# Stick-breaking stage of a retention, stick-breaking and expert layer: every second round of TensorE's work in reverse order

## The chip, the cores and the metric

The kernel runs on one core of a Trainium2 chip. The metric is the device time of one execution in microseconds (us), here the median of the runs shown. TensorE is called PE in the profile (its weight loads PEld), VectorE DVE, ScalarE ACT, GpSimd POOL and SyncE SP.

## The reference

One decoder layer on 1024 tokens of width 1024, all in float32. A combined projection gives the inputs of two head groups, retention (4 heads of 128) and stick-breaking attention (8 heads of 64). Their outputs are projected and added to the input; then 32 experts (4 for each token) are added. The change is in the stick-breaking attention, which computes for each block of 128 queries:

```python
z = einsum('bhqd,bhkd->bhqk', q_blk, kt) * scale
causal = key_pos[None, :] < q_pos[:, None]
log_one_minus = where(causal, log_sigmoid(-z), 0.0)
log_remaining = cumsum(log_one_minus, axis=3, reverse=True) - log_one_minus
weights = where(causal, exp(log_sigmoid(z) + log_remaining), 0.0)
out = einsum('bhqk,bhkd->bhqd', weights, vt)
```

Each weight is sigmoid(z) times the product of 1 - sigmoid(z) over the later keys before the query. It is also the difference of two neighbouring running products of 1 - sigmoid(z).

## The kernel before

The kernel is one program with a hand-written order for each engine and semaphores between them. Its stages are the norm and the projections with the retention woven in, the stick-breaking stage, the output projection with the router, and the loop over the experts, which takes most of the time. Each stage waits for the one before it.

**Units.** The stick-breaking stage has 96 units (`NU`, lines 383 to 394). A unit is one head, one block `i` of 128 queries and up to 512 keys. Two heads form a pair `p`; there are 4 pairs. For query blocks 0 to 3 a head has one unit of 1 to 4 key tiles of 128; for blocks 4 to 7 it has two, first the later keys (1 to 4 tiles, with the diagonal), then the first 512 keys. The two heads of a pair alternate, so that units n and n+1 (n even) are the same work for two heads. The 24 units of a pair (`PAIR`) in steps of two have 1, 2, 3, 4, 1, 4, 2, 4, 3, 4, 4, 4 key tiles.

**A unit's way.** It goes through five steps on three engines:
- `scores(n)` on PE (L1001) multiplies queries by keys for units n and n+1. Each product is split in three (high by high, high by low, low by high); each head uses 64 rows of the array. It writes bank n % 4 and bank (n+1) % 4 and increments `z_ok`. From the fifth unit on it waits for `z_not` >= n - 2 (L1007): the sigmoids of units n-4 and n-3, which had the same banks, must be done.
- `remains(n)` on ACT (L763, the operation at L768) takes the sigmoid of -z from the bank into `stick` and increments `z_not`.
- `remaining(n)` on DVE (L1433, L1446) is a scan: the running product from the last key to the first, in `rem`, which increments `z_rem`. The second unit of a query block continues from the first.
- `turn_rest(n)` on PE (L1020, L1027) transposes the 128 x 128 tiles of `rem` into bank 4 + n % 2. It waits for `z_rem` and for ACT to have emptied that bank (`z_wT` >= n - 1).
- `turned(n)` on ACT (L776, L781) copies that bank into `massT`, which has four buffers (n % 4), as 1 minus the value. Therefore it waits for `z_tr` and, from the fifth unit on, for `z_pv` >= n - 3 (L780): the values of unit n-4 must be done.
- `values(n)` on PE (L1030, L1040) multiplies differences of neighbouring value rows, `dv`, by `massT`, for units n and n+1, and adds up in bank 6 or 7. Each head writes 64 partitions. It waits for `z_wT` >= n + 2 and for the rows of `dv`, and increments `z_pv` for each unit.

The differences `dv` are made by POOL (L594) at the start of the stage from DMA copies. DVE copies each finished half of a head pair (`chain_out`, L1449) to the output. ACT copies the next pair's queries and keys in the high precision part (`pair_up`, L770, the operation at L774), DVE subtracts to get the low one (`pair_low`, L1371).

**The order.** ACT runs for n = 0, 2, ... `turned(n-4)`, `turned(n-3)`, `remains(n)`, `remains(n+1)` and at two places of a pair `pair_up` (L786 to L794). DVE runs the scans in the order of the units. PE's order is the loop that is changed (L1049 to L1056): for n = -4, -2, ..., 100 one round is `values(n-6)`, then `turn_rest(n-2)` and `turn_rest(n-1)`, then `scores(n+4)`, each where such units exist.

Of the kernel before, what the change touches and what calls it, by code (L numbers as in the profile page):

```python
# [118 lines left out]
def layer(nc, x, attn_norm_g, w_in, ret_norm_g, sb_q_norm_g, sb_k_norm_g, w_out, ffn_norm_g,  # L119
          w_router, b_router, w_gate_up, b_gate_up, w_down, b_down, consts, rope, out):  # L120
    with ExitStack() as ctx:
# [271 lines left out]
        NU = len(units)  # L393
        PAIR = NU // (SH // 2)

        def out_bank(u):
            return bank[6 + u["chain"] % 2]
# [493 lines left out]
        def _(e):  # L891
# [109 lines left out]
            def scores(n):  # L1001
                u = units[n]
                b, p = u["p"] % 2, u["p"]
                e.wait_ge(z_up, 2 * (p + 1))
                e.wait_ge(z_lo, 2 * (p + 1))
                if n >= 4:
                    e.wait_ge(z_not, n - 2)  # L1007
                queries, keys = slice(u["i"] * P, (u["i"] + 1) * P), slice(u["k0"], u["k0"] + u["w"])
                heads = ((n, slice(0, HD)), (n + 1, slice(HD, P)))
                for m, pr in heads:  # L1010
                    e.matmul(bank[m % 4][:, 0:u["w"]], q_hi[b][pr, queries], k_hi[b][pr, keys], start=True, stop=False,  # L1011
                             skip_group_check=True)
                for m, pr in heads:
                    e.matmul(bank[m % 4][:, 0:u["w"]], q_hi[b][pr, queries], k_lo[pr, p, keys], start=False, stop=False,
                             skip_group_check=True)
                for m, pr in heads:
                    e.matmul(bank[m % 4][:, 0:u["w"]], q_lo[pr, p, queries], k_hi[b][pr, keys], start=False,
                             stop=True, skip_group_check=True).then_inc(z_ok, 1)

            def turn_rest(n):  # L1020
                u = units[n]
                e.wait_ge(z_rem, n + 1)
                if n >= 2:
                    e.wait_ge(z_wT, n - 1)
                for t in range(u["n"]):
                    at = u["at"] + t * P
                    mm = e.transpose(bank[4 + n % 2][:, t * P:(t + 1) * P], rem[:, u["row"], at:at + P], ident)  # L1027
                mm.then_inc(z_tr, 1)

            def values(n):  # L1030
                u = units[n]
                e.wait_ge(z_wT, n + 2)
                e.wait_ge(z_dv, u["i"] + 1)
                if u["chain"] >= 2:
                    e.wait_ge(z_out, u["chain"] - 1)
                cols = slice(u["i"] % HT * P, (u["i"] % HT + 1) * P)
                for t in range(u["n"]):
                    for m, pr in ((n, slice(0, HD)), (n + 1, slice(HD, P))):
                        h = units[m]["h"]
                        mm = e.matmul(out_bank(u)[pr, cols], dv[:, u["k0"] // P + t, h * HD:(h + 1) * HD],  # L1040
                                      massT[m % 4][:, t * P:(t + 1) * P], start=u["diag"] and t == 0,
                                      stop=u["last"] and t == u["n"] - 1, skip_group_check=True)
                        if t == u["n"] - 1:
                            mm.then_inc(z_pv, 1)
# [2 lines left out]
            e.wait_ge(r_mix, NT)  # L1047
            e.wait_ge(r_state, NT)
            for n in range(-4, NU + 6, 2):  # L1049
                if n >= 6:  # L1050
                    values(n - 6)
                if 2 <= n < NU + 2:
                    turn_rest(n - 2)
                    turn_rest(n - 1)
                if n + 4 < NU:
                    scores(n + 4)  # L1056

            e.wait_ge(wo_in, 16)
# [61 lines left out]
            for j in range(NT - 1):  # L1120
                n = NT - 1 - j
# [661 lines left out]
```

## Time and profile before

| | |
|---|---|
| median of 3 runs | 2201.78 us (2200.51 to 2202.93) |
| the profiled execution's own time | 2200.3 us |
| its span, first to last instruction | 2198.4 us |
| granted PE clock, mean | 0.989 |
| PE busy | 97% of the span |
| DVE, ACT, POOL busy | 58%, 35%, 16% |
| stick-breaking stage, first scores to last values | 396.6 to 519.5 us of the span |

The busy shares are means over the whole span. A wait is given with the engine and line that released it. "PEclk" is the share of full speed that PE's clock was granted. "issue" as a releaser means that the profile shows nothing that the engine waited for.

### The profile page before, as it was taken

To read this page: it belongs to the slowest core of one execution; us is meant where nothing else is said; L and a number is where in the kernel's file an instruction comes from. 1 tells how busy PE (TensorE), PEld (TensorE's weight loads), DVE (VectorE), ACT (ScalarE), POOL (GpSimd) and SP (SyncE) were. 2 spreads that over 40 slices of the span, in tenths; PEclk is the share of its full clock that TensorE was granted. 3 is DMA by queue.
4 is the path that set the end of the run, shared out by engine and by line. 5 is a ranking of instruction groups with operands and counts; after the bars stand their busy time and mean duration, and the time that the engine had idled before them with its cause. 6 is when DMAs were issued, how large, how long until landed. Compare 5 with 4: busy or idle time off the path is not lost.

```text
span 2198.4 us, 42048 instructions
## 1 busy us (share of the span) xinstructions
PE 2130.8 (97%) x16443; PEld 1912.0 (87%) x16444; DVE 1274.7 (58%) x2580; ACT 765.8 (35%) x1369; POOL 346.7 (16%) x243
## 2 busy tenths in 40 slices
PE   7999999899979999999999999999999999999997
PEld 6978888677868999899989999989999999999996
DVE  6434534787366665456656655655566665666654
ACT  4143134577222333233333333332333333333332
POOL 3100300200010211111112112111211111212121
PEclk9999999999989999999999999999999999999998
DMA  5221221303365988778879887887898887999983
GB/s 178 95 88 58 96 90 45 116 2 133 136 218 177 315 306 307 241 263 310 311 264 315 307 307 264 308 296 258 310 316 308 307 305 258 317 325 330 315 286 92
DMA packets 257783, 509.59 MB, mean 232 GB/s; under 512 B 7466, under 2 KB 44510, under 8 KB 257438
## 3 DMA queue, kind: packets, MB, share of 16 engines
q1 hardware_dynamic: 234220, 451.95, 57.5%
q0 software_dynamic: 21968, 51.67, 9.6%
q10 hardware_dynamic: 1536, 5.15, 0.7%
q8 instruction: 41, 0.67, 0.1%
q14 instruction: 18, 0.15, 0.0%
HBM read 473.09 MB, written 33.55 MB: 230 GB/s over the span
## 4 chain that ended last, share of the span: by engine, by line
PE 95%; DVE 2%; issue 1%; DMA 1%; POOL 0%; ACT 0%; ACTq 0%; SPq 0%; POOLq 0%; DVEq 0%
PE bank L1217 46%; PE bank L1197 16%; PE bank L928 14%; PE bank L1205 3%; PE bank L1027 2%; PE bank L1040 2%; PE bank L1074 1%; PE bank L1140 1%; PE bank L1076 1%; PE bank L1075 1%; PE bank L1133 1%; PE bank L1011 1%; PE bank L1182 1%; PE bank L1146 1%; PE bank L936 1%
## 5 line engine op out<-in xcount | busy, mean ns | idle before, releaser
L1217 PE MATMUL bank<-hx,ring 128*128 128x140 f32 (+1 forms) x8192 | 1021.9, 287 | 7.5 <-DVEq L1659 7.5
L1217 PEld LDWEIGHTS bank<-hx,ring 128*128 128x128 f32 x8192 | 1015.0, 197 | 10.3 <-DVEq L1659 7.7
L1197 PE MATMUL bank<-work_r,hx_r 128*128 128x512 f32 x1024 | 335.1, 408 | 0.0
L1698 DVE TENSOR_TENSOR mix_r<-ring,work_r 128x1024 fp32r<-128x1024 f32 x256 | 305.1, 1223 | 41.0 <-ACT work_r L853 40.9
L870 ACT ACTIVATE hx<-hx 128x168 f32<-128x168 f32 x256 | 88.0, 344 | 595.8 <-DVE hx L1714 595.6
L1714 DVE TENSOR_SCALAR hx<-bank,small 128x168 f32<-128x168 f32 x256 | 100.3, 392 | 298.6 <-PE bank L1217 289.3
L853 ACT ACTIVATE work_r<-ring 128x1024 fp32r<-128x1024 f32 x256 | 257.7, 1042 | 0.0
L1197 PEld LDWEIGHTS bank<-work_r,hx_r 128*128 128x128 f32 x1024 | 188.1, 189 | 43.8 <-issue 10.4
L1197 PE MATMUL bank<-mix_r,hx_r 128*128 128x512 f32 x512 | 200.1, 391 | 0.0
L630 POOL DMA_INDIRECT out_x<-hx,small x32 | 52.0, 1625 | 659.5 <-ACT hx L863 621.2
L861 ACT ACTIVATE hx<-bank,small 128x512 f32<-128x512 f32 x64 | 44.0, 688 | 313.9 <-PE bank L1146 167.2
L597 POOL DMA_INDIRECT hx<-xn_scratch,small x33 | 33.9, 1029 | 574.1 <-issue 568.0
L876 ACT ACTIVATE hx_r<-hx 128x128 fp32r<-128x128 f32 x256 | 78.8, 308 | 109.0 <-DVE hx L1724 109.0
L928 PE MATMUL bank<-hx_r,mix_r 128*128 128x512 f32 x480 | 112.5, 393 | 3.7 <-DVE hx_r L1308 3.7
L1197 PEld LDWEIGHTS bank<-mix_r,hx_r 128*128 128x128 f32 x512 | 96.1, 188 | 21.0
L928 PE MATMUL bank<-hx_r,work_r 128*128 128x512 f32 x480 | 113.7, 394 | 0.0
L928 PEld LDWEIGHTS bank<-hx_r,mix_r 128*128 128x128 f32 x480 | 89.5, 188 | 23.3 <-issue 5.1
L1619 DVE TENSOR_TENSOR work<-hx,cst 128x3072 bf16<-128x3072 f32 x32 | 107.3, 3352 | 0.0
L928 PEld LDWEIGHTS bank<-hx_r,work_r 128*128 128x128 f32 x480 | 89.7, 188 | 20.2 <-issue 1.9
L633 POOL DMA_INDIRECT out_x<-hx,small x64 | 100.7, 1573 | 19.5 <-issue 19.5
L1716 DVE TENSOR_SCALAR hx<-bank,small 128x168 f32<-128x168 f32 x256 | 98.1, 383 | 0.0
L1633 DVE TENSOR_TENSOR hx<-bank,small 128x512 f32<-128x512 f32 x66 | 42.6, 686 | 86.1 <-PE bank L1140 86.1
(244 smaller groups left out, 2346.8 us busy)
## 6 DMA issues: line engine op xcount, KB each, us to landing
ring<-in_w_gate_up SPq DMA_DIRECT2D x128, 2048.0 KB, 12.9
ring<-in_w_down SPq DMA_DIRECT2D x64, 2048.0 KB, 13.1
mix<-in_w_in SPq DMA_DIRECT2D x14, 1024.0 KB, 5.0
work<-in_w_in SPq DMA_DIRECT2D x14, 1024.0 KB, 5.0
ring<-in_x SPq DMA_DIRECT2D x8, 512.0 KB, 6.0
hx<-in_w_out SPq DMA_DIRECT2D x1, 4096.0 KB, 14.1
work<-in_x ACTq DMA_DIRECT2D x8, 512.0 KB, 4.6
out_x<-work SPq DMA_DIRECT2D x8, 512.0 KB, 4.4
```

Of the source, the lines that this page charges most:

```text
L633: e.indirect_dma_start(out=out_quarters, in_=y_o[:, r], in_offset=None, compute_op=ALU.add, out_offset=bass.IndirectOffsetOnAxis(ap=idx_sc ...
L853: e.activation(dn_hi[:, nh, k:k + 2], dn_ring[:, k:k + 2, nh * CH:(nh + 1) * CH], ACT.Copy).then_inc(c_hi, 1)
L870: e.activation(sg[:, f % 2], g1[:, f % 2], ACT.Sigmoid, scale=GALPHA).then_inc(m_sig, 1)
L876: e.activation(hid_hi[:, f], hid[:, f, 0:P], ACT.Copy).then_inc(h_hi, 1)
L928: mm = e.matmul(dst, lhs, rhs, start=k == 0 and (xs is x_hi and ws is w_hi), stop=k == KD - 1 and ws is w_lo)
L1197: mm = e.matmul(bank[2 + t][:, :], h[:, k], w[:, t, k], start=False, stop=k == KD - 1 and w is dn_lo, skip_group_check=True)
L1205: e.matmul(bank[7][quarter_rows(j), r * 2 * P:(r + 1) * 2 * P], hid[:, k, P + r * OV:P + (r + 1) * OV], dn_ring[:, k, j * 2 * P:(j + 1) * ...
L1217: mm = e.matmul(bank[f % 2][:, part * CAP:part * CAP + w], gu_ring[:, k, f * 256 + part:(f + 1) * 256:2], xT[:, k, 0:w], start=k == 0, sto ...
L1619: e.tensor_tensor(hot, pos_s.unsqueeze(2).to_broadcast([P, NT, NH * P]), slot_at.unsqueeze(1).to_broadcast([P, NT, NH * P]), ALU.is_equal) ...
L1698: e.tensor_tensor(dn_lo[:, nh, k:k + 2], dn_ring[:, k:k + 2, nh * CH:(nh + 1) * CH], dn_hi[:, nh, k:k + 2].bitcast(F32), ALU.subtract).the ...
L1714: e.tensor_scalar(g1[:, b], bank[b][:, 0:CAP], be[:, f:f + 1], GLIM, ALU.add, ALU.min)\
L1716: e.tensor_scalar(u1[:, b], bank[b][:, CAP:2 * CAP], be[:, 8 + f:9 + f], GLIM + 1.0, ALU.add, ALU.min).then_inc(m_up, 1)
```

## The change

In every second round (n = -2, 2, 6, ...) PE does its three kinds of work in the reverse order: scores first, then the turns, then values. In the other rounds nothing changes. The units that a round handles and all instructions and waits are the same. What ACT, DVE, POOL and SP do, and their order, is unchanged.

```diff
             for n in range(-4, NU + 6, 2):
-                if n >= 6:
+                back = n % 4 == 2
+                if back and n + 4 < NU:
+                    scores(n + 4)
+                if not back and n >= 6:
                     values(n - 6)
                 if 2 <= n < NU + 2:
                     turn_rest(n - 2)
                     turn_rest(n - 1)
-                if n + 4 < NU:
+                if back and n >= 6:
+                    values(n - 6)
+                if not back and n + 4 < NU:
                     scores(n + 4)
```

## Rows read from the trace of the kernel before

**Rows 1.** The page: busy time by engine, and the chain that ended last by line.
```profile
PE 2130.8 (97%) x16443; PEld 1912.0 (87%) x16444; DVE 1274.7 (58%) x2580; ACT 765.8 (35%) x1369; POOL 346.7 (16%) x243
...
PE bank L1217 46%; PE bank L1197 16%; PE bank L928 14%; PE bank L1205 3%; PE bank L1027 2%; PE bank L1040 2%; PE bank L1074 1%; PE bank L1140 1%; PE bank L1076 1%; PE bank L1075 1%; PE bank L1133 1%; PE bank L1011 1%; PE bank L1182 1%; PE bank L1146 1%; PE bank L936 1%
```

**Rows 2.** Waits of PE, 380 to 760: us in total, times, longest.
```profile
PE bank L1040 <- POOL ring L594: 4.1, 1, 4.1
```

**Rows 3.** Windows, three pairs: length; PE, PEld, DVE, ACT, POOL busy; clock, DMA share, GB/s.
```profile
418.02:446.56 28.54, 28.38 (x290) 20.95 (x288) 25.00 (x29) 21.16 (x51) 0.00 (x0) 1.00 0.01 2
446.56:475.10 28.54, 28.30 (x290) 20.96 (x288) 24.75 (x29) 21.18 (x51) 0.00 (x0) 1.00 0.01 2
475.10:503.80 28.70, 28.49 (x292) 20.95 (x288) 23.53 (x27) 19.56 (x50) 0.00 (x0) 1.00 0.01 1
```

**Rows 4.** Timeline: start, length, engine, line, work, count, idle before. Rounds of PE.
```profile
441.01 0.19 PEld L1011 LDWEIGHTS bank<-ring_r 64*128 64x128 f32 x2 [0.17 <-issue]
...
441.57 0.64 PEld L1040 LDWEIGHTS bank<-work,ring 128*64 128x64 f32 x12
...
448.61 0.85 PEld L1040 LDWEIGHTS bank<-ring 128*64 128x64 f32 x16 [0.36 <-issue]
...
449.63 0.86 PEld L1027 LDWEIGHTS bank<-cst,work 128*128 128x128 f32 x8 [0.17 <-DVE work L1446]
...
450.33 1.09 ACT L781 ACTIVATE ring<-bank 128x512 f32<-128x512 f32 x2 [1.44 <-PE bank L1027]
450.66 0.19 PEld L1011 LDWEIGHTS bank<-ring_r 64*128 64x128 f32 x2 [0.17 <-issue]
...
451.30 1.10 ACT L768 ACTIVATE work<-bank 128x512 f32<-128x512 f32 x2
451.55 0.42 PEld L1040 LDWEIGHTS bank<-work,ring 128*64 128x64 f32 x8 [0.36 <-ACT ring L781]
```

**Rows 5.** Timeline of the weight loads, router behind eight full-width turns.
```profile
559.02 0.38 PEld L1096 LDWEIGHTS bank<-work,small 128*32 128x32 f32 x16 [0.17 <-issue]
```

**Rows 6.** Timeline of ACT, operations that follow each other without idle time.
```profile
441.66 1.09 ACT L768 ACTIVATE work<-bank 128x512 f32<-128x512 f32 x2
442.61 1.08 ACT L774 ACTIVATE ring_r<-ring 128x1024 fp32r<-128x1024 f32 x1
443.56 0.47 ACT L781 ACTIVATE work<-bank 128x128 f32<-128x128 f32 x2
443.87 0.71 ACT L768 ACTIVATE work<-bank 128x256 f32<-128x256 f32 x2
...
447.44 0.69 ACT L781 ACTIVATE work<-bank 128x256 f32<-128x256 f32 x2
447.96 0.94 ACT L768 ACTIVATE work<-bank 128x384 f32<-128x384 f32 x2
```

**Rows 7.** Timeline of the stage's first twenty microseconds.
```profile
403.22 12.36 POOL L594 TENSOR_TENSOR ring<-ring 128x512 f32<-128x512 f32 x8 [6.03 <-DMA ring<-ring]
...
412.21 4.45 DVE L1446 TENSOR_TENSOR_SCAN work<-work,cst 128x512 f32<-128x512 f32 x2
...
418.02 0.20 PEld L1040 LDWEIGHTS bank<-work,ring 128*64 128x64 f32 x4 [0.25 <-ACT ring L781]
```

**Rows 8.** Timeline of the stage's end.
```profile
509.18 2.46 DVE L1446 TENSOR_TENSOR_SCAN work<-work,cst 128x512 f32<-128x512 f32 x2
...
518.43 1.04 PE L1040 MATMUL bank<-ring 128*64 128x128 f32 x16
...
519.55 0.69 DVE L1452 COPY mix<-bank 128x512 f32<-128x512 f32 x1 [2.68 <-PE bank L1040]
```

**Rows 9.** Windows of the first part of the stage (columns as rows 3).
```profile
400.00:404.00 4.00, 0.90 (x10) 0.59 (x8) 3.77 (x4) 2.66 (x6) 0.78 (x1) 0.91 0.89 256
404.00:408.00 4.00, 3.03 (x14) 2.30 (x16) 0.14 (x1) 1.32 (x4) 4.00 (x4) 0.50 0.85 245
...
416.00:420.00 4.00, 3.20 (x24) 2.05 (x24) 4.00 (x5) 2.59 (x8) 0.00 (x0) 1.00 0.23 90
```

## The prediction, made before the changed kernel was run

> **What bounds the kernel now.** I read the page's busy shares first: PE is busy 97% of the span and holds 95% of the chain that ended last; the lines of the stage that is changed, L1011 to L1040, have about 2% each [rows 1]. So PE time counts everywhere. The list of waits then says whether the stage is PE's: PE's longest wait there for another engine is 4.1 us, once, for the value differences that POOL makes [rows 2]. From 418.02 on one head pair takes 28.54, 28.54, 28.70 us, in which PE is busy 28.4, DVE 25.0, ACT 21.2 [rows 3]. The stage is PE's own, with ACT idle a quarter of the time. That idle time is between ACT's work, not spare: the question is what ACT waits for under the new order.
>
> **The change part by part.** Call the units' two-by-two steps V (values), T (turns), S (scores). Before, each round is V T S. After, rounds alternate V T S and S T V. No instruction is added or removed; SP, POOL and DVE queues keep their order and nothing of them is moved. There are 24 double rounds, 6 a pair. Prices of a step of n key tiles [rows 4]: V has 4n instructions of 0.85/16 = 0.053, so 0.213n; T has 2n of 0.86/8 = 0.107, also 0.213n; S is 3 x 128n columns, with 0.89 us for 4 tiles (450.66 to 451.55) and 0.56 for 2 (441.01 to 441.57), so 0.16n + 0.25. V to T and T to S each leave a hole of 0.17 in the weight loads.
>
> *Gain.* Of a double round's two V-T, two T-S and two S-V junctions, one each of V-T and T-S and S-V go over into V-V, T-V, S-S, S-T. Same-kind neighbours cost nothing: the two turns of a step, with waits between them, are eight loads in 0.86 without a hole [rows 4]. T-V is not in the trace; its nearest row is full-width turns followed by column tiles in the router, hole 0.17 [rows 5], which I take (from 0 to 0.36). S-T is not there either: I take the 0.25 of S-V, between 0 and 0.36. The gain is a S-V and a V-T or T-S, 0.42 a double round, 10 us in all, if PE finds its data.
>
> The Trainium skill's page "TensorEngine Tiling (Array Packing)", section Key Properties, says that changing the tiling mode, not just the tile, drains TensorE. The trace agrees in that the holes of 0.17 stand exactly where 128x64, 128x128 and 64x128 tiles meet [rows 4, 5]. By that rule alone the time would fall by the 10 us above.
>
> *Loss.* Two waits of ACT and PE now close a ring. (1) Mass tiles: ACT's turned(m) waits until the values of unit m-4 are done (z_pv, L780), as there are four buffers. (2) Score banks: scores(m) waits for the sigmoids of units m-4 and m-3 (z_not, L1007). ACT's order is fixed: turned of two units, remains of two units, and so on (L786 to 792). Take n divisible by 4. V(n) now stands last in its round, behind S(n+10) and T(n+4). So:
> - turned(n+4) can't start before V(n) is done; queued behind it on ACT are turned(n+5), remains(n+8), (n+9), turned(n+6), (n+7), remains(n+10), (n+11);
> - S(n+14), now first in its round, waits for remains(n+11); T(n+8) is queued behind it, and V(n+4) behind that.
> From V(n) to V(n+4), one double round, there are thus eight ACT operations, then S, T and V of one round on PE, one after the other with nothing beside them. Before, V came first in every round and S last, and ACT's eight ran beside PE: in [rows 4] the remains are issued at 451.30, after the S at 450.66 has begun, so an S right behind it would have stood.
>
> Ring for a pair. ACT start to start for two operations of 1, 2, 4 tiles is 0.31, 0.52, 0.95 [rows 6]; 3 tiles by interpolation 0.74. A pair's twelve steps have 1,2,3,4,1,4,2,4,3,4,4,4 tiles, so two of each of 1, 2, 3 and six of 4: 2 x (0.31+0.52+0.74) + 6 x 0.95 = 8.84, for the two kinds 17.7. The last operation of each eight lasts on 0.12 to 0.14 after its slot (1.09 against 0.95): 0.8. PE's part of the six: S of the odd steps, 22 tiles, 22 x 0.16 + 6 x 0.25 = 5.0; T of the even steps, 14 tiles, 14 x 0.213 + 6 x 0.17 = 4.0; V of the same, 3.0, plus 0.32 each from its last issue to ACT (0.27 for the last matmul, 0.07 to start; a turn shows the same: loads from 449.63, four of them 0.43, ACT at 450.33, so 0.27 behind) = 1.9; ACT's end to PE's next load 0.13 (450.33 + 1.09 to 451.55) x 6 = 0.8. Sum 17.7 + 0.8 + 5.0 + 4.0 + 3.0 + 1.9 + 0.8 = 33.2. ACT also finds the second turns not quite there in four of six cycles, where the two operations before them are short (counted from V's end, after one of 128 and one of 256 columns ACT is ready at 0.83, while PE has four tiles of V, the hole and four turns before it, and delivers at 1.39: 0.5 us; three times 0.1): 0.8. So 34.0 a pair, against 28.6: +5.4. DVE needs 25.0 of it and is not last in the middle of the stage. ACT's two copies of a pair (L774, 0.95 each) stand behind remains(n+11), where ACT would idle anyway during S, T, V: nothing.
>
> Start. Before, PE idles 4.1 us up to 404.9 for the first value difference (POOL from 403.22, eight of 12.36/8 = 1.55 [rows 7]). After, S(10) and T(4) come ahead of V(0) and fall into that hole; the first scans behind it start some 1.2 us earlier. But V(2) needs the second difference (406.3), and T(11) the scans that POOL's work slows (4.45 for two, against 2.46 in [rows 8]): they would end about 415.5, not 416.66. Then: T(11) turned and ready 416.35, its ACT and two 512-wide remains to 417.9, S 0.13 + 0.89, T 0.60, V(8) 0.21 + 0.32: ready at 420.05. Before it was ready at 418.02 + 0.53 = 418.55 [rows 7]. Start: +1.5.
>
> Middle, from V(8) to V(80): 3 x 34.0 = 102.0 against 85.8 [rows 3]: +16.2.
>
> End. The last scores are gone, and the ring opens: one cycle of 6.0 (V(80) to V(84)); then the last four 512-wide scans (2.46 for two, first input 1.4 in) let T(93) run at 4.0, V(88), V(90), T(94) and T(95), V(92), V(94) follow to 9.4. 15.4 against 518.43 + 1.04 + 0.08 - 418.55 - 85.8 = 15.2 [rows 8]: +0.2.
>
> Sum +17.9 on the profiled execution's own 2200.3 (span 2198.4 plus 1.9 around it): 2218.2. The median of the runs is 1.5 above that execution, so the forecast is **2219.7 us**. All that follows (output projection, experts) starts later by the same and is unchanged.
>
> **The rivals.**
> (a) *The junctions win.* The ring has slack that I don't see, PE remains the bound: 24 x 0.42 = 10 less, DVE's 25.0 being still below 26.0: about 2191.7. For it: the holes, and ACT idle a quarter. Against: the waits stand in the code at exactly the distances above, and S, T, V of every second round have nothing of ACT beside them. It decides for faster only where the ring is under 28.5 a pair, 5 below a sum that is made of measured durations.
> (b) *Only the score wait counts.* If V's delay cost nothing, PE would stand at S for what ACT lacks: from the end of T, turned and two remains 0.2 + 0.6 + 1.1 + 0.1 = 2.0 against S 0.9, 1.1 in a wide double round, less 0.42; averaged over the narrow ones about 0.3 x 24: 2209.
> (c) *The clock falls.* PE was granted 0.91 and then 0.50 around the four microseconds that it stood [rows 9]. In the new stage it stands up to 1.7 a double round and is busy 28.4 of 34.0, 84%. At 416 to 420, busy 3.20 of 4, the clock was at 1.00 [rows 9], so I expect the high level. At half speed the 13.9 of S, T and V per pair would double: +50, about 2270.
> (d) *Nothing is seen*: gain and ring cancel, 2201.8.
>
> **How the numbers follow.** Forecast 0.84, (a) 0.05, (b) 0.05, (c) 0.04, (d) 0.02. Bounds of the forecast: no stall of ACT (-0.8), S-T at 0 (-1.5) and T-V at 0 (-1.0) a pair give -3.3 x 3.8 = -12; S-T and T-V at 0.36 (+1.8) with 0.1 more for each of the hand-overs (+1.2) give +11. I reach less far down than up at both ends, since they need all to fall together, down to (b): 2209 to 2231. No change that can be told here is within 0.2% (4.4 us): faster 0.05, same 0.02, slower 0.93.
>
> **What would show it.** In the changed trace a middle pair takes about 34 us with PE busy about 28 minus holes; ACT waits for PE's values (L1040), not for turns (L1027), once a double round, some 2.2 to 2.6 us each, 1 less where a copy of L774 fills it; PE's scores or their loads (L1011) wait for ACT's remains (L768) once a double round, the largest wait of PE in the stage; weight loads V-V and S-S show no hole, T-V 0.17, S-T about 0.25. Before V(0), S(10) and T(4) have run. I am wrong if a pair takes under 28.5, if PE's waits on L768 are missing, if ACT's turned starts before V's end, or if the granted clock in 420 to 530 is not 1.00.

## The result, and the profile after

The changed kernel takes 2228.35 us (median of 4 runs, 2220.77 to 2231.47) against 2201.7 before; the ratio is 1.0116, 95% interval 1.0099 to 1.0134. It is slower, within the stated range of 2209 to 2231 and 8.7 us above the forecast of 2219.7. The profiled execution took 2220.77 us, against 2218.2 forecast for it.

The windows of the same three head pairs, V(8) to V(80), in the changed kernel (columns as in [rows 3]):

```profile
419.77:454.57 34.80, 28.03 (x289) 21.23 (x288) 26.33 (x30) 21.45 (x50) 0.00 (x0) 1.00 0.01 2
454.57:489.40 34.83, 27.93 (x291) 21.26 (x290) 25.25 (x29) 21.45 (x50) 0.00 (x0) 1.00 0.01 1
489.40:524.20 34.80, 27.98 (x291) 21.30 (x291) 23.19 (x27) 19.50 (x48) 0.00 (x0) 1.00 0.01 2
```

A head pair takes 34.8 us where it took 28.6 [rows 3]. PE, DVE and ACT are busy about as long as before, but now none of them is busy all the time: what is new is waiting. The list of waits of the stage (396 to 545), us in total, times and longest:

```profile
ACT work L781 <- PE bank L1040: 50.8, 23, 2.7
...
PE bank L1011 <- ACT work L768: 24.2, 27, 1.4
```

Before, PE's longest wait was the one for POOL [rows 2]. Now ACT waits 23 times for values and PE 27 times for ACT's sigmoids. The page of the profile says it too: the chain that ended last, 95% PE and 0% ACT before, has

```profile
PE 93%; DVE 2%; ACT 2%; issue 2%; DMA 1%; POOL 0%; ACTq 0%; DVEq 0%; POOLq 0%
```

One double round of the changed kernel in the timeline (columns as in [rows 4]; `...` stands for rows left out). V, T and S are the steps values, turns and scores; L1040 is V, L1027 T, L1011 the first part of S, L781 ACT's `turned` and L768 its `remains`:

```profile
454.57 0.20 PEld L1040 LDWEIGHTS bank<-work,ring 128*64 128x64 f32 x4 [0.17 <-issue]
...
454.74 0.91 PEld L1040 LDWEIGHTS bank<-ring 128*64 128x64 f32 x16
...
455.10 0.66 ACT L781 ACTIVATE work<-bank 128x256 f32<-128x256 f32 x2 [2.14 <-PE bank L1040]
455.65 0.88 ACT L768 ACTIVATE work<-bank 128x384 f32<-128x384 f32 x2
455.81 0.86 PEld L1027 LDWEIGHTS bank<-cst,work 128*128 128x128 f32 x8 [0.17 <-issue]
...
456.51 1.09 ACT L781 ACTIVATE ring<-bank 128x512 f32<-128x512 f32 x2
456.84 0.19 PEld L1011 LDWEIGHTS bank<-ring_r 64*128 64x128 f32 x2 [0.17 <-issue]
...
457.48 1.09 ACT L768 ACTIVATE work<-bank 128x512 f32<-128x512 f32 x2
...
458.69 0.22 PEld L1011 LDWEIGHTS bank<-ring_r 64*128 64x128 f32 x2 [1.32 <-issue]
...
459.62 0.42 PEld L1027 LDWEIGHTS bank<-cst,work 128*128 128x128 f32 x4 [0.36 <-DVE work L1451]
```

V stands last in its round (454.57), with the next V behind it without a hole. ACT starts on `turned` at 455.10, after 2.14 idle. Its eight operations follow each other up to 458.57 with no idle time listed between them. PE's second S loads at 458.69, 0.12 behind the last of them. The second S of each double round waits so. The six of one pair (weight loads, timeline):

```profile
493.50 0.21 PEld L1011 LDWEIGHTS bank<-ring_r 64*128 64x128 f32 x2 [1.32 <-issue]
...
499.91 0.21 PEld L1011 LDWEIGHTS bank<-ring_r 64*128 64x128 f32 x2 [1.52 <-issue]
...
505.64 0.22 PEld L1011 LDWEIGHTS bank<-ring_r 64*128 64x128 f32 x2 [0.90 <-issue]
...
511.06 0.21 PEld L1011 LDWEIGHTS bank<-ring_r 64*128 64x128 f32 x2 [1.18 <-issue]
...
516.79 0.22 PEld L1011 LDWEIGHTS bank<-ring_r 64*128 64x128 f32 x2 [1.43 <-issue]
...
522.64 0.21 PEld L1011 LDWEIGHTS bank<-ring_r 64*128 64x128 f32 x2 [1.38 <-issue]
```

They add up to 7.73 us, and a pair is 6.2 longer, so 1.5 is given back elsewhere. The weight loads of the middle pair say where. If each step is counted up to the first load of the next, V goes from 9.69 to 9.09, T from 10.00 to 9.99, and S from 8.85 to 15.75, of which 7.80 are these waits. So V gives back 0.6 and S 0.9. At the stage's end DVE copies the last values at 539.91, against 519.55 [rows 8]:

```profile
539.91 0.69 DVE L1457 COPY mix<-bank 128x512 f32<-128x512 f32 x1 [3.09 <-PE bank L1040]
```

That is 20.4 us later, and the profiled executions differ by 20.5: nothing is given back or lost behind the stage.

**The spread.** The four runs of the changed kernel lie 10.7 us apart. Their spans and mean granted clocks:

```
run   us       span    clock   (1 - clock) x span, us
1     2220.77  2218.9  0.989   24
2     2231.47  2229.6  0.983   38
3     2228.04  2226.1  0.985   33
4     2228.65  2226.8  0.985   33
```

The slower runs have a lower clock: 9 more in the last column goes with 7.2 to 7.9 us more of span, 14 more with 10.7. The profile shows run 1, the one with the highest clock; the other three were not profiled.

### The profile page after: what moved, and what is told of

It reads as the page before. It is cut to its first block, busy times and chain, and to the rows that moved or that the text cites. A ratio compares the mean times of both kernels' runs of the same rounds, so it can differ in the third digit from the quotient of the medians.

```text
span 2218.9 us, 42048 instructions
## 1 busy us (share of the span) xinstructions
PE 2129.1 (96%) x16443; PEld 1913.0 (86%) x16444; DVE 1277.9 (58%) x2580; ACT 766.4 (35%) x1369; POOL 348.6 (16%) x243
## 4 chain that ended last, share of the span: by engine, by line
PE 93%; DVE 2%; ACT 2%; issue 2%; DMA 1%; POOL 0%; ACTq 0%; DVEq 0%; POOLq 0%
PE bank L1222 46%; PE bank L1202 16%; PE bank L928 14%; PE bank L1210 3%; PE bank L1079 1%; PE bank L1145 1%; PE bank L1081 1%; PE bank L1080 1%; ACT work L768 1%; PE bank L1027 1%; PE bank L1040 1%; PE bank L1138 1%; PE bank L1187 1%; PE bank L1151 1%; PE bank L936 1%
```

## The experiments

Times are medians, with the ratio to the kernel before on the same chip and its 95% interval. "A pair" is the distance from V(8 + 24p) to the next in the profile, at a granted clock of 1.00. Edits are shown against the changed kernel where nothing else is said, and `...` marks lines left out. Line numbers move by a few with the edits.

**The change once more.** No edit.

> The changed kernel once more, unaltered. Four executions of it spread from 2220.8 to 2231.5 us, with mean granted clocks 0.989 (the fastest) to 0.983 (the slowest), where the kernel before spreads 2.4 us. Theory: the ring costs 18 to 20 us in every execution, and what varies beyond that is the clock, so each execution above 2222 should show a mean clock under 0.989, and the profile, if it falls on one, should show the granted clock under 1.00 in 420 to 545. Rival: the spread is the ring itself, with waits of different length at the same clock; then times differ at equal clock.

Measured: 2225.78 us (2224.04 to 2229.25), 1.0105 (1.0089 to 1.0120); the profiled execution has a span of 2223.6 and a clock of 0.986. Its loads of V(32) and V(56) in the timeline are

```profile
456.90 0.20 PEld L1040 LDWEIGHTS bank<-work,ring 128*64 128x64 f32 x4 [0.17 <-issue]
...
491.73 0.20 PEld L1040 LDWEIGHTS bank<-work,ring 128*64 128x64 f32 x4 [0.17 <-issue]
```

34.83 apart, as in the first profile. But V(32) is at 456.90, not 454.57. The windows before it, first the changed kernel's first profile, then this one:

```profile
404.00:412.00 8.00, 5.84 (x37) 4.18 (x35) 6.66 (x5) 4.16 (x9) 8.00 (x6) 0.64 0.94 339
412.00:420.00 8.00, 6.05 (x62) 4.22 (x60) 8.00 (x6) 3.34 (x9) 4.89 (x3) 1.00 0.58 232
...
428.00:436.00 8.00, 5.89 (x65) 4.55 (x62) 5.53 (x7) 5.28 (x13) 0.00 (x0) 1.00 0.00 1
```

```profile
404.00:412.00 8.00, 6.55 (x36) 4.81 (x37) 4.96 (x5) 4.13 (x9) 8.00 (x6) 0.50 0.94 338
412.00:420.00 8.00, 6.91 (x57) 4.93 (x54) 7.85 (x6) 3.25 (x9) 4.90 (x3) 0.79 0.57 227
...
428.00:436.00 8.00, 6.40 (x57) 5.35 (x57) 5.01 (x5) 4.35 (x10) 0.00 (x0) 0.79 0.00 1
```

The clock was lower for longer at the start and fell once more at 428 to 436. So a pair has the same length in both executions, and 2.3 of the 4.7 us between them have come about up to V(32), where the clock is lower. The other 2.4 lie behind V(56). Of these, 1.6 come between the first loads of L1187 (714.6 and 717.9) and of L1210 (727.0 and 731.9), in the loop over the experts, where the windows are, first profile and this one:

```profile
716.00:720.00 4.00, 4.00 (x20) 3.27 (x19) 2.93 (x8) 3.04 (x5) 0.00 (x0) 1.00 0.95 359
720.00:724.00 4.00, 4.00 (x22) 3.17 (x21) 2.10 (x2) 0.47 (x1) 0.00 (x0) 1.00 0.04 12
```

```profile
716.00:720.00 4.00, 2.05 (x8) 1.58 (x9) 3.42 (x12) 0.71 (x3) 0.00 (x0) 0.90 0.98 356
720.00:724.00 4.00, 4.00 (x14) 3.16 (x13) 3.35 (x4) 2.79 (x3) 0.00 (x0) 0.67 0.50 186
```

The clock is lower there too, but PE also stands longer, so how much of the 1.6 is the clock's isn't shown. The theory of the spread holds for the 2.3 up to V(32), and the ring costs the same in both profiles. But the spread is not the change's alone: in this comparison 15 runs of the kernel before lie between 2201.0 and 2207.4, at mean clocks from 0.989 to 0.985. The medians here are 21.8 us apart, near the 20.4 that the stage grew by, where those of the first comparison were 26.7 apart. Whether PE's new idle times make the clock fall more often stays open. The mean clock of the changed kernel's eight runs is 0.9856, that of these 15 runs 0.9869. But the next experiment, in which PE waits as long, has 0.9868 in its four runs.

**Scores first, values where they were.**

```diff
                 if back and n + 4 < NU:
                     scores(n + 4)
-                if not back and n >= 6:
+                if n >= 6:
                     values(n - 6)
...
-                if back and n >= 6:
-                    values(n - 6)
```

> Only half of the change: in every second round scores come first, then values, then turns. V(n) is no longer behind S(n+10) and T(n+4), so the ring through the mass tiles is open; only the scores' wait for ACT's sigmoids stays. Theory of the forecast, as it was written (rival b): that wait alone costs little, about 2209 us. Rival, from the chain T, turned, two remains, S, V, T, V, T of one double round priced with the rows of before: 35.5 us a pair, so no faster than the changed kernel, 2218 to 2228.

Measured: 2225.98 us (2225.01 to 2228.67), 1.0104 (1.0089 to 1.0120), as slow as the whole change. A pair in its windows:

```profile
446.51:481.60 35.09, 28.65 (x291) 21.11 (x289) 25.45 (x29) 21.62 (x50) 0.00 (x0) 1.00 0.00 1
```

35.09 against 35.5 worked out. ACT waits in this kernel for turns, not for values:

```profile
ACT work L781 <- PE bank L1027: 11.1, 6, 2.4
```

The scores' wait alone is enough for the whole loss; the forecast's size for it, 2209, was wrong.

**Values late, scores where they were.**

```diff
-                if back and n + 4 < NU:
-                    scores(n + 4)
...
-                if not back and n + 4 < NU:
+                if n + 4 < NU:
                     scores(n + 4)
```

> The other half: in every second round turns come first, then values, then scores. S stays last, so it has its old distance from ACT's sigmoids; V(n) is behind T(n+4), so turned(n+4) waits for it, but S(n+10) and T(n+4) do not stand between. As many changes of tile shape as before the change. If the ring needs both halves: within 3 us of the kernel before (2199 to 2205). If V's delay alone closed it (ACT held at turned(n+4)): 2212 or more.

Measured: 2204.13 us (2200.89 to 2207.88), 1.0004 (0.9995 to 1.0013). A pair:

```profile
439.40:468.22 28.82, 28.67 (x289) 20.98 (x288) 25.03 (x29) 21.32 (x51) 0.00 (x0) 1.00 0.01 1
```

V's delay alone costs 0.3 a pair or less (28.82 against 28.54), and nothing that can be told in the whole time.

**Eight mass tiles.**

```diff
-        massT = [region(work, 8192, 2, CH)[:, m] for m in range(2)] + [region(ring, 7168, 2, CH)[:, m] for m in range(2)]
+        massT = [region(work, 8192, 2, CH)[:, m] for m in range(2)] + [region(ring, 7168, 2, CH)[:, m] for m in range(2)] \
+            + [region(ring, 10240, 4, CH)[:, m] for m in range(4)]
...
-                if n >= 4:
-                    e.wait_ge(z_pv, n - 3)
+                if n >= 8:
+                    e.wait_ge(z_pv, n - 7)
```

`massT[n % 4]` becomes `massT[n % 8]` at both places.

> The changed kernel with eight mass tiles instead of four (the four new ones lie in a part of SBUF that is free in this stage), and turned(n) waits for the values of unit n-8. The ring through the mass tiles is gone, the order of all engines is that of the change. If that ring is the bound: back to the scores' wait alone, about 2209 by the forecast's rival (b). If the chain through the scores' wait is as long (34.5 us a pair by the rows of before): no gain, 2216 to 2228, and ACT's idle time moves from the releaser PE L1040 to PE L1027.

Measured: 2221.99 us (2220.24 to 2222.95), 1.0084 (1.0070 to 1.0098). A pair, and the waits of ACT and PE in it:

```profile
444.42:478.53 34.11, 27.73 (x289) 21.24 (x288) 25.55 (x30) 21.54 (x51) 0.00 (x0) 1.00 0.01 1
```

```profile
ACT ring L782 <- PE bank L1028: 9.8, 10, 1.5
...
PE bank L1012 <- ACT work L769: 6.4, 6, 1.3
```

ACT now waits for turns (L1028 here), as the second theory said, and PE waits for sigmoids as before. Opening the ring through the mass tiles gives 0.7 a pair (34.8 to 34.1). The way through turns, ACT and scores is nearly as long as the ring, so it took over.

**ACT turned too.** The edit is to ACT's loop (L786 to L794), and `before_act` makes it alone in the kernel before.

```diff
+                late = n % 4 == 2
-                if n >= 4:
+                if n >= 4 and not late:
                     turned(n - 4)
                     turned(n - 3)
                 if n < NU:
                     remains(n)
                     remains(n + 1)
...
+                if n >= 4 and late:
+                    turned(n - 4)
+                    turned(n - 3)
```

> The changed kernel, with ACT's order turned in the same rounds: where PE takes scores first, ACT takes the two remains before the two turned (four mass tiles as before). S(n+6) then needs sigmoids that do not queue behind turned(n-1). Theory: the whole loss comes from ACT's order standing against PE's, and with it gone the saved changes of tile shape appear, 0.42 a double round, PE 26.1 a pair with DVE's 25.0 just below it: 2192 to 2198. Rival: DVE, or turned(n+4) still waiting for V(n), holds the pair at 28.5 or more: 2201 and up.

> The same with eight mass tiles. If the four tiles no longer matter once ACT's order is turned: the same time as with four within 2 us. If V(n) last in its round still holds ACT: 3 us or more faster than with four.

> Control: PE's order of the kernel before, with only ACT's order turned in every second round. Theory (the gain of the turned pair comes from PE's tile shapes, not from ACT's order): the time of the kernel before within 3 us. Rival: ACT's order itself was late before, then this is faster by 3 us or more; or ACT now comes late with turned and it is slower.

Measured: with four mass tiles 2207.2 us (2204.27 to 2208.67), 1.0020 (1.0011 to 1.0029); with eight 2196.76 us (2193.66 to 2202.72), 0.9978 (0.9967 to 0.9988); ACT's order alone, on PE's old one, 2202.17 us, 0.9996 (0.9987 to 1.0005). A pair of the first, and ACT's longest wait in it:

```profile
442.97:472.86 29.89, 27.56 (x290) 21.31 (x289) 24.86 (x29) 20.91 (x50) 0.00 (x0) 1.00 0.01 1
```

```profile
ACT work L781 <- PE bank L1044: 9.0, 6, 1.8
```

A pair of the second:

```profile
437.90:464.94 27.04, 26.46 (x290) 20.96 (x289) 24.54 (x29) 21.34 (x51) 0.00 (x0) 1.00 0.01 2
```

With ACT's order following PE's, 4.9 of the 6.2 us that a pair had lost are gone (34.8 to 29.9). What is left is V last in its round: ACT still waits six times a pair for values (L1044 here), and here the four mass tiles cost 2.85 a pair, where they had cost 0.7. With both gone the pair is 1.5 shorter than before the change, and this version is 0.2% faster than the kernel before, clear of the noise. ACT's order alone does nothing (2202.17, and a pair of 28.54), and eight tiles alone do nothing either (the control below), so the 1.5 comes from PE's order.

**The cheaper mixture, and the tiles alone.** Scores first and values where they were, with ACT turned too and four mass tiles; and the kernel before with eight mass tiles. Both edits are those shown above.

> Every second round scores, values, turns (values ahead of the turns as before), with ACT's order turned in the same rounds, four mass tiles. V(n) is ahead of T(n+4) again, so turned(n+4) should find its mass tile free, and S no longer waits behind turned. Changes of tile shape: V T S | S V T has five instead of six in a double round, in holes 0.96 us against 1.18. Theory: 28.6 - 6 x 0.22 = 27.3 a pair, 2196 to 2200, without more memory. Rival: ACT or DVE is late and the pair stays at 28.5 or more, 2202 and up.

> Control: the kernel before with eight mass tiles and nothing else. Before, V always runs ahead of the turns that its mass tile is wanted for, so the tiles are free in time: the time of the kernel before within 2 us. If it is faster by 3 us or more, the gain of the turned pair with eight tiles is partly that of the tiles alone.

Measured: 2203.86 us (2200.82 to 2208.44), 1.0010 (1.0001 to 1.0019), and 2203.35 us (2200.24 to 2207.3), 1.0004 (0.9995 to 1.0012). The control did as expected. The mixture missed its forecast of 2196 to 2200. Two neighbouring loads of V in its trace, V(32) and V(56):

```profile
441.21 0.20 PEld L1044 LDWEIGHTS bank<-work,ring 128*64 128x64 f32 x4 [0.37 <-issue]
...
469.34 0.20 PEld L1044 LDWEIGHTS bank<-work,ring 128*64 128x64 f32 x4 [0.36 <-issue]
```

28.13 a pair, 0.4 less than before instead of 1.3. Counted up to the first load of the next step, V is at 9.69 as before, T at 9.74 instead of 10.00, and S at 8.70 instead of 8.85. So the gain forecast for S behind S, 0.22 a double round, came to 0.15 a pair. Two of the six second S have idle times of 0.27 and 0.28 ahead of them, which takes 0.55 of it. Where the first S is narrow, there was little to save: S of 2 and of 4 tiles take 1.39 together, and 0.56 + 0.89 = 1.45 apart. With 0.4 a pair no gain can be told in the whole time. The median is even 1.6 us higher; the mean clock of these eleven runs is 0.9858, against 0.9874 in the 23 of the kernel before.

## Why the prediction was right, and where it was not

- *What bounds the kernel now*: right. PE's own time in the stage was 28.6 a pair, and ACT's idle time was what broke.
- *Start*: forecast V(8) 1.5 later; its loads are at 419.77, 1.75 after 418.02. S(10) and T(4) ran ahead of V(0) (404.87, against 404.94 before), as forecast.
- *Middle*: forecast 34.0 a pair, +16.2 in three; measured 34.8, 104.43 - 85.78 = +18.65.
- *End*: forecast +0.2, measured 539.91 - 524.20 against 519.55 - 503.80, -0.04. Sum +20.4 against +17.9: direction and mechanism right, the ring priced 2% short. The term that was short is ACT's. In the middle pair its six eights last 20.05 together, where the forecast has 17.7 + 0.8 and 0.8 for second turns that come late. The other parts of the ring take 34.83 - 20.05 = 14.8, forecast 14.7. Part of ACT's excess isn't listed as idle time: the two sigmoids of one tile at 479.32 are followed by the next operation after 0.55, where 0.31 is their price.
- *The signs*: ACT waits for V's values 2.14 to 2.68 a time, and 1.43 where a copy fills the gap, forecast 2.2 to 2.6 and 1 less. PE's wait for the sigmoids is its largest in the stage. S-T is 0.36, where the forecast had 0.25.
- *What makes the loop*: only half right. The forecast made the loss a ring of two waits and gave the scores' wait alone, its rival (b), 2209. With only that wait there the time is 2226 and a pair 35.1; with only V's delay it is that of the kernel before. The step that failed is in (b): the wait was worked out for a wide double round and then cut to "about 0.3" for narrow ones. But the turned and remains on this way are those of the odd steps, of which five of six have 4 tiles. The whole way priced by the same rows, us a pair: ACT 10.5 + 0.8, S 5.0, V of both steps 7.7, T of the even steps 3.0 and the first turn of the odd ones 2.4, three holes of 0.17 a double round 3.1, hand-overs from PE to ACT and back 2.0 + 0.8, in all 35.3 (the expectation of the run had 35.5, and 35.09 was measured). With V behind V one of the holes is gone: 34.3, where eight mass tiles measured 34.1. The ring through the mass tiles is a second way of nearly the same length (33.2 and its stalls, forecast), and takes 0.7 more.
- *The gain from tile shapes*: real, but 0.25 a double round, (28.54 - 27.04)/6, not 0.42. A look at the best version's loads shows one reason, two S of four tiles one behind the other, up to the turns:

```profile
449.14 0.18 PEld L1016 LDWEIGHTS bank<-ring_r 64*128 64x128 f32 x2 [0.17 <-issue]
...
449.71 0.19 PEld L1016 LDWEIGHTS bank<-ring_r 64*128 64x128 f32 x2
...
450.73 0.64 PEld L1032 LDWEIGHTS bank<-cst,work 128*128 128x128 f32 x6 [0.36 <-issue]
...
451.53 1.29 PEld L1045 LDWEIGHTS bank<-ring 128*64 128x64 f32 x24 [0.17 <-issue]
```

  From 449.14 to 450.73 is 1.59 for two S. In the old order it is 2 x 0.89 = 1.78, and the forecast had 0.64 + 0.89 = 1.53. The junction itself is free: from 449.48 on the matmuls of both S start 0.23 to 0.24 apart, across the border too. But three of these make 0.70 for the second S, where the forecast had taken 0.64, so what an S loses by its junctions is 0.19 of its 0.89 and not 0.25. T-V has the 0.17 that was taken from the router. So the shapes give 0.36 for two such S. By steps the 1.5 of this version are V 9.69 to 8.77 and S 8.85 to 8.23, with T as before (10.04). The forecast's 2.5 were 1.0 from V's side, which nearly came, and 1.5 from S's. One of S's junctions to T has a hole of 0.80 instead of 0.36, which takes 0.4 of that.
- *Slips in the working*: the sentence on the gain names four new junctions for three old ones; both S-V go, as its 0.42 has it. And 0.27 + 0.07 is 0.34, not 0.32. Neither moves the sum by more than 0.1 a pair.
- *The clock*: the forecast expected 1.00 between 420 and 530. The first profile has it, the second has 0.79 at 428 to 436. Rival (c) had the clock fall for the whole stage, which no profile shows. The forecast took one profiled execution at 0.989 for all and had no term for executions at a lower clock. The first median (2228.35) is that of four runs of which three were at 0.985 or under, while the one at 0.989 came out at 2220.77. The median is 8.7 above the forecast. Of that, 2.6 is what the profiled execution took too long, and 6.1 comes from the median lying 7.6 above that execution, where the forecast had 1.5. That the median still lies within the range is in part luck: its upper end, 2231, was worked out from holes and hand-overs alone. Against the kernel before on the same chip, the second comparison's +21.8 leaves 3.9 over the 17.9 forecast, of which 2.5 are the ring's and the start's.

## What to carry to other kernels

When an order written out by hand is changed on one engine, follow each wait to the other engines' own orders: an operation that is moved forward past one other may overtake the answer that it needs, which stands in a queue that was not turned with it. Price each way from a step back to the same step of the next round on its own, with the sizes of exactly the steps on it, before calling one wait harmless. And where a changed order loses by such waits, turning the other engine's order in the same rounds and giving the buffers one more round can bring out the gain that it was made for.

## What the runs showed of the hardware

Steps of one kind behind each other have no gap: the matmuls of two S of four tiles (pairs of 64x128 with 512 columns) start 0.23 to 0.24 us apart within the steps and across their border. The second S therefore takes 0.70 us, while an S between two changes of tile shape takes 0.89. The weight loads of T wait 0.36 behind an S of 512 columns, as those of V do [rows 4]. V to T, T to S and T to V show 0.17 where nothing else is late.

One core's executions of one kernel differ by more than the first three runs of the kernel before had suggested (2.4 us apart). Fifteen runs of the kernel before lie 6.4 us apart, at mean clocks of 0.985 to 0.989, and the first four of the changed one 10.7, at 0.983 to 0.989. The longer ones have the lower clock in these tables and in most, not all, of the other kernels: the five runs of `eight_mass` lie 2.7 apart at 0.986 to 0.987, with no such order.
